# Another order of the three token tiles in the first norm of a hybrid decoder step

## The reference, cut to what matters

```python
tok = concat([meta, x_prompt, x_sample])            # 280 rows of 1024
u   = rmsnorm(tok, norm_mix) @ w_in                 # 1024 x 3584, seven groups of 512 columns
y   = token_mixers(u)                               # gated conv (groups bg, cg, hv) and
                                                    # gated linear recurrence (q, fx, iv, og)
h   = tok + y @ w_out                               # then the meta rows are dropped
h   = h + moe(rmsnorm(h, norm_ffn))                 # top 4 of 32 experts, 1024 -> 2048 -> 1024
out = rmsnorm(h, norm_final)

def rmsnorm(x, g):
    return x * rsqrt(mean(x * x, axis=-1) + EPS) * g
```

## Time and profile before

| | |
|---|---|
| runs | 1129.71, 1126.74, 1130.45 us; median 1129.71 |
| the profiled execution's own time | 1130.05 us |
| its span, first to last instruction | 1128.2 us |
| TensorE busy | 1051.5 us, 93% |
| VectorE, ScalarE, GpSimd busy | 285.1, 183.2, 27.0 us |
| read from HBM | 427.50 MB, 382 GB/s over the span |
| expert weights, issues | 184 of 2048 KB and 16 of 1024 KB |

### The profile page before, as it was taken

The page is one execution under the profiler, slowest core; times in us unless marked ns, Lnnn a source line. Parts: engine busy times, 40 slices in busy tenths (PEclk is TensorE's granted clock), DMA queues, the critical chain, the costliest instruction groups (busy, mean ns, idle before and its releaser), DMA issues.

```text
span 1128.2 us, 13104 instructions
## 1 busy us (share of the span) xinstructions
PE 1051.5 (93%) x5365; PEld 467.9 (41%) x5365; DVE 285.1 (25%) x517; ACT 183.2 (16%) x422; POOL 27.0 (2%) x64
## 2 busy tenths in 40 slices
PE   7999998999999999989898999998989899999996
PEld 6767855343343333424242424342434343433432
DVE  5657535312130202111121212120202020201133
ACT  2561014220110110102020202010101010100103
POOL 3000013000000000000000000000000000000000
PEclk9999999999999999999999999999999999999999
DMA  9942475899999999999999999999999999999994
GB/s 305 359 158 75 167 251 233 325 429 428 428 426 426 429 428 428 428 429 429 429 429 428 429 428 428 428 429 429 428 429 429 428 429 429 428 428 428 427 421 158
DMA packets 50034, 431.46 MB, mean 382 GB/s; under 512 B 5086, under 2 KB 15878, under 8 KB 24304
## 3 DMA queue, kind: packets, MB, share of 16 engines
q1 hardware_dynamic: 47984, 428.15, 91.2%
q0 software_dynamic: 752, 2.56, 0.7%
q10 hardware_dynamic: 1264, 0.28, 0.1%
HBM read 427.50 MB, written 3.48 MB: 382 GB/s over the span
## 4 chain that ended last, share of the span: by engine, by line
PE 59%; DMA 36%; DVE 2%; ACT 1%; issue 1%; SPq 1%; DVEq 0%
DMA ring<-in_expert_w 35%; PE ps L1781 20%; PE ps L1835 16%; PE ps L1416 6%; PE ps L1706 4%; PE ps L1394 2%; PE ps L1542 2%; PE ps L1717 2%; ACT mem L774 1%; PE ps L1484 1%; PE ps L1814 1%; PE ps L1719 1%; DMA ring<-in_x_prompt 1%; SPq L420 0%; PE ps L1403 0%
## 5 line engine op out<-in xcount | busy, mean ns | idle before, releaser
L1781 PE MATMUL ps<-ring,mem 128*64 128x512 f32 x2048 | 464.4, 603 | 49.1 <-DMA ring<-in_expert_w 49.1
L1781 PEld LDWEIGHTS ps<-ring,mem 128*64 128x64 f32 x2048 | 154.6, 138 | 347.1 <-issue 346.3
L1835 PE MATMUL ps<-ring,mem 128*64 128x512 f32 x1024 | 225.3, 594 | 4.9 <-ACT mem L792 2.0
L1224 DVE TENSOR_TENSOR mem<-mem,ps 128x1024 f32<-128x1024 f32 x30 | 36.6, 1221 | 468.7 <-PE ps L1717 431.9
L1835 PEld LDWEIGHTS ps<-ring,mem 128*64 128x64 f32 x1024 | 84.2, 137 | 134.2 <-issue 132.1
L784 ACT ACTIVATE mem<-mem 128x512 f32<-128x512 f32 x32 | 20.2, 630 | 540.1 <-DVE mem L1289 540.1
L1416 PE MATMUL ps<-mem,ring 128*128 128x266 f32 (+1 forms) x320 | 77.6, 399 | 2.0 <-DVE mem L910 1.5
L1717 PE MATMUL ps<-mem 128*128 128x512 f32 (+1 forms) x180 | 76.5, 611 | 0.0
L1416 PEld LDWEIGHTS ps<-mem,ring 128*128 128x128 f32 x320 | 60.9, 194 | 16.6 <-issue 3.9
L1289 DVE TENSOR_SCALAR mem<-ps 128x512 f32<-128x512 f32 x32 | 22.1, 691 | 154.2 <-PE ps L1781 154.2
L1706 PEld LDWEIGHTS ps<-mem 128*128 128x128 bf16 x840 | 47.4, 97 | 12.2 <-issue 12.2
(11 more groups left out here) (288 smaller groups left out, 521.3 us busy)
## 6 DMA issues: line engine op xcount, KB each, us to landing
ring<-in_expert_w SPq DMA_DIRECT2D x184, 2048.0 KB, 26.9
ring<-in_expert_w SPq DMA_DIRECT2D x16, 1024.0 KB, 23.6
ring<-in_w_in SPq DMA_DIRECT2D x6, 2048.0 KB, 22.2
ring<-in_w_out SPq DMA_DIRECT2D x2, 2048.0 KB, 11.0
ring<-in_w_in SPq DMA_DIRECT2D x2, 1024.0 KB, 8.1
ring<-in_state_rec SPq DMA_DIRECT2D x4, 512.0 KB, 10.6
out<-ring SPq DMA_DIRECT2D x4, 512.0 KB, 10.6
out<-mem SPq DMA_DIRECT2D x5, 256.0 KB, 4.6
```

The lines of the kernel that those rows point to most:

```text
L1224: dve.tensor_tensor(h3[:, m], h3[:, m], ps[:, 4 + 2 * m:6 + 2 * m, :].rearrange("p a n -> p (a n)"), ALU.add)\
L1781: done = mm(ps[CAP * e:CAP * e + CAP, b, :], xgT4[:, k, t, CAP * e:CAP * e + CAP], ring[:, slot[e], col:col + HALF], start=False, stop=(t ...
L1835: done = mm(ps[CAP * e:CAP * e + CAP, 4 + half, :], actT3[:, 4 * v + t, CAP * e:CAP * e + CAP], ring[:, slot[e], col:col + HALF], start=(v ...
```

## The change

The three slabs are taken in the order 2, 0, 1 on ScalarE: small tile, prompt tile 0, prompt tile 1. The semaphore counts follow the new order. On TensorE the turns go small tile, prompt tile 0; then the gains are turned and the factors of these two tiles are spread; then prompt tile 1 is turned and its factor spread by itself. On VectorE the diagonals of the small tile and of tile 0 come first, then the gains and the product of the small tile with `norm_mix`, then the diagonal of tile 1, then as before the copy of all factors and the scalings. The semaphore `xT_ps` is gone (the gains' `gains_ps`, which stands behind the small tile's turns, covers it), `few_sb` is new: VectorE waits for its own product before it goes on to the factors. No transfer, shape or instruction of arithmetic is added or removed.

```diff
@@ ScalarE
-            for i in range(3):
+            for nth, i in enumerate(ORDER):
                 r = TILE_ROWS[i]
                 act.wait_ge(x_in[i], 48 if i == 2 else 16)
                 act.activation(lo[0:r, i * D:(i + 1) * D], x3[0:r, i], ACT.Square, accum_out=ssq[0:r, i:i + 1])\
                     .then_inc(x_sq, 1)
-                act.wait_ge(x_sq, i + 1)
+                act.wait_ge(x_sq, nth + 1)
@@ VectorE
-            def spread_diag(i):
+            def spread_diag(nth, i):
                 r, at = TILE_ROWS[i], TILE_COL[i]
-                dve.wait_ge(root_sb, i + 1)
+                dve.wait_ge(root_sb, nth + 1)
...
-            spread_diag(0)
-            spread_diag(1)
-            spread_diag(2)
+            spread_diag(0, 2)
+            spread_diag(1, 0)
             few = xT3[:, :, 0:P0C]
             dve.wait_ge(gains_ps, 1)
             dve.tensor_copy(gains, ps[:, 7, 0:40]).then_inc(gains_sb, 1)
             dve.wait_ge(gains_sb, 1)
-            dve.wait_ge(xT_ps, 1)
-            link(dve.tensor_tensor(few, ps[:, 4, 0:KT * P0C].rearrange("p (t b) -> p t b", t=KT),
-                                   bcast(gmix.unsqueeze(2), [P, KT, P0C]), ALU.mult))
+            dve.tensor_tensor(few, ps[:, 4, 0:KT * P0C].rearrange("p (t b) -> p t b", t=KT),
+                              bcast(gmix.unsqueeze(2), [P, KT, P0C]), ALU.mult).then_inc(few_sb, 1)
+            spread_diag(2, 1)
+            dve.wait_ge(few_sb, 1)
             dve.wait_ge(spread_ps, 1)
@@ TensorE
             pe.wait_ge(ident_sb, 1)
-            for i in range(3):
+            def turn_x(i):
                 pe.wait_ge(x_in[i], 48 if i == 2 else 16)
...
-            last.then_inc(xT_ps, 1)
+                return last
+
+            def spread_of(nth, i):
+                r, at = TILE_ROWS[i], TILE_COL[i]
+                pe.wait_ge(diag_sb, nth + 1)
+                return mm(ps[:, 5, at:at + r], ones[0:r, :], diag[0:r, at:at + r], start=True, stop=True)
+
+            turn_x(2)
+            turn_x(0)
             pe.wait_ge(gain_in, 80)
             pe.transpose(ps[:, 7, 0:40], gain_rows, ident[0:40, 0:40]).then_inc(gains_ps, 1)
-            for i in range(3):
-                r, at = TILE_ROWS[i], TILE_COL[i]
-                pe.wait_ge(diag_sb, i + 1)
-                last = mm(ps[:, 5, at:at + r], ones[0:r, :], diag[0:r, at:at + r], start=True, stop=True)
-            last.then_inc(spread_ps, 1)
+            spread_of(0, 2)
+            spread_of(1, 0)
+            turn_x(1)
+            spread_of(2, 1).then_inc(spread_ps, 1)
```

More of the change, by code:

```diff
@@ L260, in build_step @@
             sem(n) for n in ("ident_sb", "own_sb", "fS_sb", "s0f_sb", "mixc_ps")]
-        gains_ps, gains_sb, x_sq, root_sb, diag_sb, spread_ps, xT_ps, xT_dve, fx_in = [
-            sem(n) for n in ("gains_ps", "gains_sb", "x_sq", "root_sb", "diag_sb", "spread_ps", "xT_ps", "xT_dve",
+        gains_ps, gains_sb, x_sq, root_sb, diag_sb, spread_ps, few_sb, xT_dve, fx_in = [
+            sem(n) for n in ("gains_ps", "gains_sb", "x_sq", "root_sb", "diag_sb", "spread_ps", "few_sb", "xT_dve",
                              "fx_in")]
```

## The result

| | before | after |
|---|---|---|
| median of 18 runs | 1129.59 us (1126.74 to 1131.79) | 1131.01 us (1129.70 to 1132.08) |
| ratio | | 1.0017, 95% interval 1.0010 to 1.0023 |
| profiled execution, own time and span | 1130.05, 1128.2 | 1129.70, 1128.0 |

The forecast was 1131.4. So the two profiles compared as wholes would say "nothing changed". The front has to be read by itself.

A forecast was written before the change was run, and what follows sets the result against it. The kernel was taken as TensorE-bound up to 352 us, then bound by the weight stream. 1130.05 + 1.74 gave 1131.8, or 1131.4 us against the median of three runs, 1129.71; range 1128.0 to 1133.8.

The forecast's parts named there:

- T: Landing time of the small tile, on which TensorE and ScalarE begin in the new order; taken as 6.7 us.
- TensorE's sum: TensorE's turns, gains and spreads after the small tile lands, priced one by one; 6.88 us in all.
- The shift at the copy and the first matmul: Front of the kernel: copy of the factors starts at 13.72 instead of 11.98, +1.74 us; first projection matmul equally later.
- Roots: ScalarE's root after each tile's square at the front, ending at 8.2, 9.6 and 10.95 us; claimed hidden behind TensorE.
- Propagation: A TensorE shift at the front moves the weight stream's start, and through it the end, by the same amount.
- The rival that it is hidden: Rival: the weight stream doesn't move and the front's shift is hidden later; 1129.7 us, chance 0.05.
- The faster rival: Rival: small tile lands early (break-even 4.96 us) and the front gains; best case -0.9, 1128.8 us, chance 0.05.
- the gains' bound: Front: gains must land before 7.88 us, since 4.10 us of TensorE lead from them to the copy.
- The clock: TensorE's rise from the 1.2 GHz level in the first projection stream; assumed to move with the stream, cost 0.
- keeps its time: Rival: clock rise in the first projection stream stays at its time; 0.85 us given back, 1130.6 us, chance 0.10.
- later: Rival: clock rises late in the first projection stream; 1.7 us on top of 1.7, 1133.1 us, chance 0.08.
- Five microseconds of turns did not raise the clock: Argument for the late clock rise: TensorE was busy from 6.98 to 11.88, yet the projection stream began slow.

The follow-up runs named there:

- turns3: Kernel before the change with 24 more turns of prompt tile 1 between the small tile's turns and the gains; ratio 1.0023 to before.
- small_early: Changed kernel with the small tile's three transfers issued at the head of SyncE's queue instead of on ScalarE's; ratio 0.9995 to before.
- warm_start: Kernel before the change with two 512-column matmuls ahead of the first turn and one of 448 in the gap behind the last spread; ratio 0.9989 to before.
- warm_again: The same kernel as warm_start, measured again on the chip of the next three runs; ratio 0.9971 to before.
- act_dve_back: Changed kernel with the order 0, 1, 2 put back on ScalarE and VectorE, TensorE still turning prompt tile 1 last; ratio 1.0013 to before.

## Why the prediction was right, step by step

- *T.* Read from packet counts and the landing of the transfer behind it as 6.7, between 5.3 and 7.4; it was 6.76 in the profiled execution. The lag of 1.2 in this reading is taken from no row: the rows show at least 1.0. The estimate of 4.1 that the prediction worked out from the Trainium skill (DMA: Bandwidth & Descriptors, sections "Queues, rings and completion order" and "Anatomy of one DMA") came 2.7 too early. The second of these sections is on transfers that GpSimd issues, and these three go out on ScalarE's queue.
- *TensorE's sum.* 6.88 from the first turn to the end of the last spread; measured 6.89 to 13.48, 6.59. As the chain counts them, small turn and tile 0 took 2.92 (2.88 forecast), the gains 0.26 (0.26), two spreads 1.27 (1.08), the turn of tile 1 1.71 (1.91), the last spread 0.44 (0.75). The release before it was 0.13 instead of 0.04.
- *The shift at the copy and the first matmul.* +1.74 forecast, +1.60 and +1.61 measured.
- *ScalarE.* Roots at 8.2, 9.6, 10.95 forecast; 8.25, 9.63, 10.98 measured. VectorE's moved products ended at 10.70, ahead of that root: hidden, as said.
- *Propagation.* Forecast whole; the rest column and turns3 show it. The rival that it is hidden is out.
- *The faster rival* had the right condition: small_early met T and the gains' bound, and the copy came at 11.60, 0.38 earlier.
- *The clock.* This is the weak step. I let the rise move with the stream and allowed for "keeps its time" and "later". It came ahead of the stream in the changed kernel's profiled execution (15.33), which no case held. So the sign of the trace's span was outside my cases although the median was not. That the rise comes at different moments in executions of one kernel is shown by warm_start and warm_again, whose first streams took 15.33 and 16.63. Over 18 runs it left the effect at 1.4 to 1.9. Whether the changed order itself raises the clock early more often (its front has 6.6 us of TensorE work without a gap; before has 7.0 with one gap of 0.19) can't be told from one trace a kernel. With the spread of the runs halved, the forecast's plain shift is not the whole of what happened, and that the median came within 0.4 of it is in part luck.
- "Five microseconds of turns did not raise the clock" was true of that execution and not a rule: turns3 and act_dve_back rose among turns.

## What to carry to other kernels

Before work is put first because it is small, ask when its data land, in the trace, by the packets of its queue: a tile of 96 KB, issued within 1.3 us of the first prompt tile's 512 KB but on another queue, landed at 6.76, some 2 us behind it (in before tile 0 was in hand by 4.73). The tile that lands first goes first, and what is put behind a late one loses its cover in full. And where one trace a kernel is at hand, compare it stretch by stretch: a clock that rises at another moment can hide, or fake, a change of 2 us.

## What the runs showed of the hardware

- The small tile (three transfers of 32, 56 and 8 KB on ScalarE's queue) landed 4.95 us behind the start of its last issue. From 2.6 to 4.0 us 0 (before) or 2 (after) packets of that queue moved, against 111 and 141 of the other queue with the prompt tiles; at the head of the other queue it was in hand at 3.65.
- The column of granted clock can read 1.00 at the front of a trace while the engine runs at half pace (5 to 7 records in 2 us against 10 or 11); count records there.
- The first projection took 15.33 us at the 2.4 GHz level and up to 17.8 where it began at 1.2; a dip near 194 us goes with about 1.5 more and comes in 5 of 14 traces. Together they could make 4 of the 5 us by which runs of the kernel before differ; that they do is not shown, with one trace of it.
- Idle TensorE time ahead of the first data can be worth filling: two matmuls of 512 columns there and one in the later gap gave the best version, 0.9971 (6 runs) and 0.9989 (11 runs) of before; without the one in the gap it was 0.9996.
